# Weight rows held since the front are used by the last expert pair instead of two earlier pairs, and the loop of periods runs one more turn

## What is computed

```python
logits = xt @ router_w + router_b
vals, idx = lax.top_k(logits, TOP_K)            # 4 of 32
combine = ...                                   # softmax of the four, 0 for the rest
for e in range(N_EXPERTS):
    gu = xt @ w1[e] + b1[e]                     # w1[e]: 1024 x 2048
    gate = jnp.minimum(gu[:, :D_FF], SWIGLU_LIMIT)
    lin = jnp.clip(gu[:, D_FF:], -SWIGLU_LIMIT, SWIGLU_LIMIT)
    glu = gate * jax.nn.sigmoid(SWIGLU_ALPHA * gate)
    out = (glu * (lin + 1.0)) @ w2[e] + b2[e]   # w2[e]: 1024 x 1024
    acc = acc + combine[:, e:e + 1] * out
```

## Time and profile before

| | us |
|---|---|
| median of 3 runs | 1020.27 |
| lowest and highest | 1020.05, 1021.27 |
| span of the profiled execution | 1016.9 |
| PE busy in it | 952.9 (94%) |
| DVE, ACT, POOL busy | 297.3, 168.3, 74.5 |
| read from HBM | 418.62 MB |

### The profile page before, as it was taken

How to read it: one execution, slowest core, us unless ns; L and a number is a source line. 1 busy time by engine, 2 the same in 40 slices (tenths; PEclk the granted TensorE clock), 3 DMA queues, 4 the chain that set the end, 5 groups by cost and what they waited for, 6 DMA issues and landing times.

```text
span 1016.9 us, 12859 instructions
## 1 busy us (share of the span) xinstructions
PE 952.9 (94%) x5424; PEld 429.7 (42%) x5424; DVE 297.3 (29%) x520; ACT 168.3 (17%) x355; POOL 74.5 (7%) x62
## 2 busy tenths in 40 slices
PE   9999999999998998989899898989999899998987
PEld 8999444343332433333243333324333334343322
DVE  5897622131303122131212222121222213131212
ACT  5355612011010101011010101002010101010012
POOL 5986000000000000000000000000000000000000
PEclk9999999999999999999999999999999999999999
DMA  9979999999999999999999999999999999999995
GB/s 320 320 309 420 364 428 431 433 425 436 423 440 422 432 431 429 433 427 436 425 436 427 432 431 426 436 427 436 427 433 433 423 434 426 435 423 434 420 422 197
DMA packets 31309, 420.49 MB, mean 414 GB/s; under 512 B 4210, under 2 KB 4754, under 8 KB 12445
## 3 DMA queue, kind: packets, MB, share of 16 engines
q1 hardware_dynamic: 30891, 418.84, 97.6%
q10 hardware_dynamic: 378, 1.10, 0.3%
HBM read 418.62 MB, written 1.49 MB: 413 GB/s over the span
## 4 chain that ended last, share of the span: by engine, by line
issue 90%; PE 9%; DMA 1%; DVE 0%; ACTq 0%; POOLq 0%; POOL 0%; DVEq 0%
PE psum L786 2%; PE psum L788 2%; PE psum L787 2%; PE psum L820 1%; PE psum L819 1%; PE psum L818 1%; DMA rows_all<-in_x_sample 1%; PE psum L705 0%; PE psum L774 0%; PE psum L795 0%; PE psum L697 0%; DVE rows_all L1947 0%; POOLq L86 0%; POOL rms L1991 0%; PE psum L764 0%
## 5 line engine op out<-in xcount | busy, mean ns | idle before, releaser
L996 PE MATMUL psum<-ring,rows_all 128*64 128x512 f32 x2012 | 462.1, 609 | 40.2 <-DMA ring<-in_exp_w 39.6
L996 PEld LDWEIGHTS psum<-ring,rows_all 128*64 128x64 f32 x2012 | 139.4, 139 | 317.4 <-issue 259.7
L1013 PE MATMUL psum<-ring,rows_all 128*64 128x512 f32 x896 | 199.5, 599 | 11.7 <-DMA ring<-in_exp_w 11.7
L1013 PEld LDWEIGHTS psum<-ring,rows_all 128*64 128x64 f32 x896 | 67.5, 138 | 134.7 <-issue 134.7
L1433 ACT ACTIVATE rows_all<-rows_all 128x512 f32<-128x512 f32 x32 | 20.1, 630 | 512.0 <-DVE rows_all L1795 512.0
L1812 DVE SCALAR_TENSOR_TENSOR y_low<-psum,gate_of,y_high 128x512 fp32r<-128x512 f32 x32 | 23.9, 751 | 244.7 <-ACT y_high L1446 244.2
L1795 DVE TENSOR_SCALAR rows_all<-psum 128x512 f32<-128x512 f32 x32 | 22.1, 692 | 197.7 <-PE psum L996 197.7
L1784 DVE TENSOR_TENSOR rows_all<-rows_all,psum 128x512 f32<-128x512 f32 x56 | 36.0, 684 | 120.2 <-PE psum L1063 120.2
L1993 POOL TENSOR_TENSOR rms<-rms,half 128x3 f32<-128x3 f32 x1 | 0.8, 850 | 910.4 <-DVE rms L1937 910.4
L1446 ACT ACTIVATE y_high<-psum,gate_of 128x512 fp32r<-128x512 f32 x32 | 22.0, 688 | 215.2 <-PE psum L1013 189.1
L889 PEld LDWEIGHTS psum<-place,x_thirds 128*128 128x128 bf16 x744 | 46.6, 97 | 13.0 <-issue 13.0
(11 more groups left out here) (273 smaller groups left out, 770.3 us busy)
## 6 DMA issues: line engine op xcount, KB each, us to landing
ring<-in_exp_w SPq DMA_DIRECT2D x53, 4096.0 KB, 30.1
ring<-in_exp_w SPq DMA_DIRECT2D x72, 2048.0 KB, 25.4
ring<-in_exp_w SPq DMA_DIRECT2D x18, 1024.0 KB, 25.5
ring<-in_w_in SPq DMA_DIRECT2D x3, 2048.0 KB, 19.8
ring<-in_w_out SPq DMA_DIRECT2D x1, 4096.0 KB, 13.0
ring<-in_exp_w SPq DMA_DIRECT2D x2, 1536.0 KB, 16.8
ring<-in_exp_w SPq DMA_DIRECT2D x5, 512.0 KB, 19.8
held<-in_exp_w SPq DMA_DIRECT2D x1, 2048.0 KB, 11.9
```

Of the source, the lines that this page charges most:

```text
L996: last = mm(psum[c * SLOTS:(c + 1) * SLOTS, bank, :], gathered_t[:, 4 * kk + j, e, :], weights, start=False, stop=(kk == 1 and j == 3), sk ...
L1013: last = mm(psum[e * SLOTS:(e + 1) * SLOTS, 4 + c, :], h_t[:, 4 * i + j, e, :], ring_w2[:, slot, e, j, c * BANK:(c + 1) * BANK], start=Fal ...
```

## The change

The same three buffers are filled, at the same points of the front, with other rows: `held` with a part of unit 0 of pair 15 (expert 30), `late` and `late_half` with a part of unit 1 of pair 15 (expert 31). So pairs 13 and 14 load their units whole, and of pair 15 unit 0 loads 2 MB and unit 1 loads 1.5 MB. Since pair 13 and 14 are now like the pairs before them, the loop runs for m = 1 to 6 and takes them in, on all engines. The sum of bytes is the same.

```diff
+    KEPT_PAIR = PAIRS - 1
...
             def load_held():
-                rows = exp_w1[0][PAIRS * 2 - 4, 0:4 * P, :]
+                rows = exp_w1[0][2 * KEPT_PAIR, 0:4 * P, :]
...
             def load_late():
-                rows = exp_w1[0][PAIRS * 2 - 6, 0:4 * P, :]
+                rows = exp_w1[0][2 * KEPT_PAIR + 1, 0:4 * P, :]
...
             def load_behind_half(pair, slot):
-                rows = exp_w1[0][bass.ds(pair * 2, 1), 0:4 * P, :]
+                rows = exp_w1[0][bass.ds(pair * 2 + 1, 1), 0:4 * P, :]
...
-                    elif half and i == 0:
+                    elif kept and i == 1:
                         load_behind_half(pair, slot)
...
-                with nc.sync.Fori(1, HALF - 2) as m:
+                with nc.sync.Fori(1, HALF - 1) as m:
...
-                h6 = reg(nc.sync, r * HALF + HALF - 2, ROUNDS * HALF)
-                load_period(h6, 1, PAIRS - 3, half=True)
                 h7 = reg(nc.sync, r * HALF + HALF - 1, ROUNDS * HALF)
-                load_period(h7, 0, PAIRS - 2, kept=True)
-                load_period(h7, 1, PAIRS - 1, last=True)
+                load_period(h7, 1, KEPT_PAIR, last=True, kept=True)
...
-                h6 = reg(nc.tensor, r * HALF + HALF - 2, ROUNDS * HALF)
-                period(h6, 1, kept=(late, late_landed, 4), half=late_half)
                 more = None
                 if isinstance(r, int):
                     pe.wait_ge(counts_ready, 1)
                     more = more_rounds(nc.tensor)
                 h7 = reg(nc.tensor, r * HALF + HALF - 1, ROUNDS * HALF)
-                period(h7, 0, kept=(held, held_landed, 2))
-                period(h7, 1, final=True)
+                period(h7, 1, final=True, kept=((held, held_landed), (late, late_landed)), half=late_half)
```

More of the change, by code:

```diff
@@ L565, in load_first, with load_period @@
                     load_w1(pair, i, i)
-            def load_period(h, b, pair, last=False, kept=False, half=False):
+            def load_period(h, b, pair, last=False, kept=False):
                 first = 4 if b else -2
@@ L965, in first_product @@
                 direct = first and isinstance(h, int)
-                own, own_landed, loads = kept or (None, None, 0)
+                own, own_landed = kept or (None, None)
                 if j == 0:
@@ L970, in first_product @@
                     if kept:
-                        pe.wait_ge(own_landed, 2 * h + loads)
+                        pe.wait_ge(own_landed, 2 * h + 2)
                 if j == 2 and half is not None:
-                    pe.wait_ge(late_half_landed, 2 * h + loads)
+                    pe.wait_ge(late_half_landed, 2 * h + 2)
                 if j == 0:
@@ L1080, in spread_tile, with period @@
                 return_rows(b, j, 6 + j % 2, True, True).then_inc(spread, 1)
-            def period(h, b, first=False, spreads=True, final=False, kept=None, half=None):
+            def period(h, b, first=False, spreads=True, final=False, kept=(None, None), half=None):
                 direct = first and isinstance(h, int)
@@ L1115, in period @@
                         pe.wait_ge(gt_read, 2 * i + j + 1)
-                    first_product(h, b, i, j, first, split=direct or second, kept=kept if i == 0 else None,
-                                  halves=final and i == 3, half=half if i == 0 else None)
+                    first_product(h, b, i, j, first, split=direct or second, kept=kept[i] if i < 2 else None,
+                                  halves=final and i == 3, half=half if i == 1 else None)
                     if spreads and (i, j) in ((0, 1), (0, 3), (1, 1)):
@@ L1214, in round_of @@
                 period(reg(nc.tensor, r * HALF + 1, ROUNDS * HALF), 0)
-                with nc.tensor.Fori(1, HALF - 2) as m:
+                with nc.tensor.Fori(1, HALF - 1) as m:
                     period(reg(nc.tensor, r * HALF + m, ROUNDS * HALF), 1)
                     period(reg(nc.tensor, r * HALF + m + 1, ROUNDS * HALF), 0)
-                h6 = reg(nc.tensor, r * HALF + HALF - 2, ROUNDS * HALF)
-                period(h6, 1, kept=(late, late_landed, 4), half=late_half)
                 more = None
@@ L1493, in round_of @@
                 period(reg(nc.scalar, r * HALF + 1, ROUNDS * HALF), 0)
-                with nc.scalar.Fori(1, HALF - 2) as m:
+                with nc.scalar.Fori(1, HALF - 1) as m:
                     period(reg(nc.scalar, r * HALF + m, ROUNDS * HALF), 1)
                     period(reg(nc.scalar, r * HALF + m + 1, ROUNDS * HALF), 0)
-                h6 = reg(nc.scalar, r * HALF + HALF - 2, ROUNDS * HALF)
-                period(h6, 1)
                 h7 = reg(nc.scalar, r * HALF + HALF - 1, ROUNDS * HALF)
-                period(h7, 0)
                 period(h7, 1, final=True)
@@ L1920, in round_of @@
                 period(reg(nc.vector, r * HALF + 1, ROUNDS * HALF), 0, 2)
-                with nc.vector.Fori(1, HALF - 2) as m:
+                with nc.vector.Fori(1, HALF - 1) as m:
                     period(reg(nc.vector, r * HALF + m, ROUNDS * HALF), 1, m * 2 + 1)
                     period(reg(nc.vector, r * HALF + m + 1, ROUNDS * HALF), 0, m * 2 + 2)
-                h6 = reg(nc.vector, r * HALF + HALF - 2, ROUNDS * HALF)
-                period(h6, 1, PAIRS - 3)
                 h7 = reg(nc.vector, r * HALF + HALF - 1, ROUNDS * HALF)
-                period(h7, 0, PAIRS - 2)
                 period(h7, 1, PAIRS - 1, final=True)
```

## The result

| | before | changed |
|---|---|---|
| median of 5 runs, us | 1020.27 | 1023.47 |
| lowest to highest, us | 1019.09 to 1021.27 | 1022.83 to 1024.49 |
| span of the profiled execution, us | 1016.9 | 1021.1 |

The changed kernel is slower: ratio 1.0034, interval 1.0023 to 1.0045, so 3.5 us (2.3 to 4.6). The forecast was 4.4 us more (1024.7), range 1023.0 to 1027.5. Each execution of these kernels lasts 1.7 to 1.9 us longer than its own span (for the profiled one of the changed kernel 1022.83 against 1021.1). So the 3.4 us between the span and the median before are not only the start and the end around the span: the profiled execution before was, by this, also about 1.6 us shorter than the median.

A forecast was written before the change was run, and what follows sets the result against it. The stream was taken to limit the loop, with PE near its limit and little reserve in the last stretch. PE 9.66 us later less 5.30 us of waits gave 4.4 us more, 1024.7 us, range 1023.0 to 1027.5.

The forecast's parts named there:

- What bounds what: The weight stream limits the loop and never pauses; from pair 15 to the last unit's end PE waits only 4.8 us.
- Step 1: Head of period 15: pair 13's second `w2` unit starts 10.85 us later, at 933.80, with two periods taking 116.86 us.
- Step 2: Pair 15's first matmul follows that `w2` unit by 9.03 us, at 942.83, so PE is 9.66 us later than before.
- Step 3: From unit 1 of pair 15 on, the queue holds the same loads at the same times, landing at 942.2.
- SP's later issues: PE's lateness delays load issues for pairs 14 and 15, 10.7 us for unit 2; queued work covers it, costed at nothing.
- Step 4: Behind pair 15's first matmul all seven waits go, 4.81 us plus 0.07 us each (0.49), giving back 5.30 us.
- Sum: At the end of the last unit: 9.66 - 5.30 = 4.4 us later, making the span 1021.3 and the median 1024.7 us.
- The clock: In the last period no long wait is left to lower PE's granted clock, so 0; one fall would cost 1.6 us.
- The loop's branch and the register load: The extra loop turn and the load of `more_i` ahead of period 15 cost 0, upper bound 1.13 us.
- Rival A: No change, 1020.3 us: the last landing sets the end and the stream carries the same bytes; chance 0.12.
- Rival B: 1026 to 1027.5 us: one clock fall (1.6 us) or branch stall (up to 1.1 us) adds to the 4.4; chance 0.08.
- Rival C: Faster, about 1018 us: short loads let the last stretch's queue run at full rate, gaining some 2.5 us; chance 0.04.

The follow-up runs named there:

- less_before: The kernel before with half of the load of unit 2 of pair 15 (2 MB) left out: 1015.43 against 1020.14 us, ratio 0.9953.
- less_after: The changed kernel with half of the load of unit 2 of pair 15 (2 MB) left out: 1023.57 us against 1020.14 before, ratio 1.0034.
- fill_small_after: The changed kernel with 17 filler matmuls (3.96 us) before pair 15's first product on TensorE: 1026.58 us; the changed kernel beside it 1023.10.
- written_out_again: Second run of the changed kernel with pairs 13 and 14 written out instead of looped: 1024.07 us, ratio 1.0039 to the kernel before.

## Why the prediction was right, and where it was off

*What bounds what* held: the stream sets the end before (less_before, 4.7 us of 4.9), PE sets it now (less_after 0, fill_small_after 3.5 of 3.9). Two readings were loose: of the eight waits seven lie in the stretch of 72.07 us (4.81 us), the eighth, 1.13 us, right ahead of it; and the stream isn't full to its very end (before, DMA share 0.86 from 995 to 1000 us, 0.36 from 1000 to 1002, 0.70 from 1002 to 1004).

*Step 1*, the head of pair 15 comes 10.85 us later: from landing to landing over two periods 116.87 us, forecast 116.86.

*Step 2*, 9.03 us to the first matmul on `held`, without a wait: 9.02.

*Step 3*, the stream beyond it unchanged, and SP's later issues covered: no wait is left, the weights are in by 1004 us in both traces, and less_after shows that nothing of the end hangs on them.

*Step 4* was mis-sized. The waits went, all seven. But a wait cost more than its gap plus 0.07 us. Two halves of a unit with a wait between them are 3.65 + 3.65 us of records and the gap; the unwaited unit at 975.55 is 7.09. So a wait within a unit gives back its gap and 0.21 us (two of them), one ahead of the last unit 0.17 (997.66 + 3.65 - 1001.14), the four others 0.07: 0.87 instead of 0.49, and the last unit's records are 0.05 shorter. From the first matmul of pair 15 to the end of the last unit it was 66.29 us, and I had 72.07 - 5.30 = 66.77; the last 0.05 us of the difference are in no single term.

*Sum*: 9.66 - 5.78 = 3.9 us instead of 4.4, which is what the traces differ by (188.30 and 192.18 us). The measured 3.5, 3.5 and 3.6 us (the ratios 1.0034, 1.0034 and 1.0035 of three measurements) have intervals from 2.2 to 4.8 us, so 3.9 fits; between it and them nothing was found but scatter. The forecast span, 1021.3, is nearer to the 1021.1 measured than the working deserves, and that is luck: the stream stood 0.9 us earlier in this execution, and the time behind PE's last matmul was 1.3 us longer. The 3.4 us added to the span are more than the start and the end around it (1.7 to 1.9 us in each execution). That does no harm, since the same 3.4 us stand between the span and the median before.

*Cover.* The clock: the granted clock is 1.00 from the first product of pair 15 to the end of the last unit in every one of these traces. The loop's branch and the register load: 0, as taken from the row. The stall of which the Trainium skill warns for a taken branch to a target that hasn't been fetched ("Runtime: NRT & Kernel Launch", Instruction fetch mechanics) shows neither in a gap (none at 823.02, where the loop turns back, and none at 939.89, where it is left) nor in written_out_again (0.3 us). *Rival A* failed where it was said to: PE's lateness of 9.66 us is over the reserve. The Roofline section of the Trainium skill's "Perfetto Trace Analysis" calls a kernel below the ridge point memory-bound. Taken for the whole of this kernel that leaves the time where it was, since the 418.62 MB read are unchanged; it moved by 3.5 us. The kernel before by itself agrees with it: less_before gained 4.7 us from 2 MB less. *Rival B* had no part: no fall of the clock, no stall. *Rival C* neither: the last landings didn't matter any more.

## What to carry to other kernels

In a kernel whose stream of weights doesn't pause, moving the rows that are held since the front from one stage to another doesn't shorten the stream; it only decides when the engine gets its data. Count the waits of the engine from the place in question to the end: they are the reserve. A delay that is smaller than the reserve costs nothing, and what goes beyond it comes out in the time. Put the short loads early enough that the engine can work off what it gets late, not all of them into the last stage.

## What the runs showed of the hardware

Two things had not been expected. The time behind PE's last matmul, with the final stores, has two lengths. The changed kernel's window behind it (us, busy times as above, clock, DMA share, GB/s):

```profile
1013.76:1021.10 7.34, 0.01 (x1) 0.00 (x0) 2.62 (x4) 1.24 (x2) 0.00 (x0) 0.85 0.44 163
```

It is 7.3 us there and 6.9 to 7.4 us in eleven other profiles, but 6.1 us in that of before and 6.0 in that of written_out_again; the engines' work in it is the same. The difference lies behind the issue of the last store (3.1 us before, 4.3 in the changed kernel). In the two short ones the two stores that SP issues take 1.60 us from first to last issue, in the others 0.99 to 1.40; why is open. So 1.3 us of a difference between two spans can be this. And in these traces a wait of PE costs more than the idle time that the timeline shows, by 0.07 us between different groups of matmuls and 0.21 us within one.
